# The opening loads of a two-layer encoder kernel: a part of their own behind a barrier, or the head of SyncE's main program

## The reference

```python
def trunk(x, mem, weights):
    for l in range(DEPTH):                                   # 2 layers
        y = parallel_mixer(x, pos, w_in[l], ...)             # windowed attention beside an mLSTM
        x = layer_norm(ALPHA * x + y, ln1_g[l], ln1_b[l])
        y = memory_cross_attention(x, mem, wq_mem[l], wkv_mem[l], wo_mem[l])
        x = layer_norm(ALPHA * x + y, ln2_g[l], ln2_b[l])
        y = grouped_moe(x, router_w, router_bias, w_gate[l], w_up[l], w_down[l])
        x = layer_norm(ALPHA * x + y, ln3_g[l], ln3_b[l])
    return x

def parallel_mixer(x, pos, w_in, ...):
    u = x @ w_in                                             # 1024 -> 2832 columns
    aq, ak, av = u[..., :512], u[..., 512:640], u[..., 640:768]
    ...                                                      # gates: the last 16 columns
```

## Time and profile before

| | |
|---|---|
| executions | 2495.45, 2500.0, 2500.74 us |
| median | 2500.0 us |
| profiled execution | 2492.09 us, of which the span from the first to the last instruction is 2490.4 us |
| PE busy | 2198.6 us (88%) |
| DVE busy | 1317.7 us (53%) |
| ACT busy | 989.8 us (40%) |
| DMA over the span | 386.56 MB, mean 155 GB/s |

### The profile page before, as it was taken

How to read it: one execution, slowest core, us unless ns; L and a number is a source line. 1 busy time by engine, 2 the same in 40 slices (tenths; PEclk the granted TensorE clock), 3 DMA queues, 4 the chain that set the end, 5 groups by cost and what they waited for, 6 DMA issues and landing times.

```text
span 2490.4 us, 35127 instructions
## 1 busy us (share of the span) xinstructions
PE 2198.6 (88%) x13178; PEld 1861.2 (75%) x13178; DVE 1317.7 (53%) x2054; ACT 989.8 (40%) x1642; POOL 199.4 (8%) x241
## 2 busy tenths in 40 slices
PE   5799898998988779999698989899898887999993
PEld 5778875988878757777587887598887875777772
DVE  2476367452153556556767726845215445665567
ACT  2255466223231335455334536622324123554552
POOL 0000011000000222000200000100000022210004
PEclk9899998999998689999899999899999877999997
DMA  3531121122100469999611112023210036999995
GB/s 146 203 106 35 35 85 38 66 102 68 65 29 26 163 239 371 377 382 372 226 60 34 35 35 85 24 80 102 68 51 35 26 132 228 372 378 382 378 369 199
DMA packets 78244, 386.56 MB, mean 155 GB/s; under 512 B 10393, under 2 KB 11433, under 8 KB 43305
## 3 DMA queue, kind: packets, MB, share of 16 engines
q1 hardware_dynamic: 54608, 327.70, 35.1%
q0 software_dynamic: 10448, 31.44, 3.5%
q10 hardware_dynamic: 13064, 25.75, 2.8%
HBM read 338.78 MB, written 46.07 MB: 155 GB/s over the span
## 4 chain that ended last, share of the span: by engine, by line
PE 74%; DVE 14%; ACT 6%; issue 3%; DMA 2%; ACTq 0%; POOL 0%; DVEq 0%; POOLq 0%
PE bank L1923 35%; PE bank L2341 9%; PE bank L2315 8%; PE bank L2305 7%; PE bank L1939 2%; PE bank L2050 2%; PE bank L2221 2%; DVE weight_slots_parts L1292 2%; PE bank L2290 1%; PE bank L2040 1%; ACT weight_slots_parts L855 1%; PE bank L2069 1%; PE bank L2254 1%; ACT x_transposed L995 1%; PE bank L2180 1%
## 5 line engine op out<-in xcount | busy, mean ns | idle before, releaser
L1923 PE MATMUL bank<-weight_slots_parts,x_transposed_parts 128*128 128x256 f32 x2496 | 469.7, 290 | 14.2 <-ACT mixer_region L918 13.9
L1923 PEld LDWEIGHTS bank<-weight_slots_parts,x_transposed_parts 128*128 128x128 f32 x2496 | 401.6, 198 | 15.9 <-ACT mixer_region L918 15.1
L1729 DVE TENSOR_TENSOR weight_slots_parts<-weight_slots,mixer_region_parts 128x2048 fp32r<-128x2048 f32 x140 | 323.7, 2331 | 85.7 <-ACT mixer_region_parts L1129 85.5
L1292 DVE TENSOR_TENSOR weight_slots_parts<-weight_slots,weight_slots_parts 128x2048 fp32r<-128x2048 f32 x58 | 132.9, 2292 | 300.7 <-ACT weight_slots_parts L855 300.2
L1923 PE MATMUL bank<-x_transposed_parts,weight_slots_parts 128*128 128x256 f32 (+1 forms) x1024 | 267.0, 349 | 24.4 <-issue 13.2
L1129 ACT ACTIVATE mixer_region_parts<-weight_slots 128x2048 fp32r<-128x2048 f32 x140 | 261.0, 1909 | 20.5 <-ACT x_transposed L1196 18.2
L2341 PE MATMUL bank<-weight_slots,x_transposed 128*128 128x512 f32 x560 | 246.4, 593 | 0.0
L1923 PEld LDWEIGHTS bank<-x_transposed_parts,weight_slots_parts 128*128 128x128 f32 x1024 | 183.9, 197 | 48.5 <-issue 14.5
L2315 PE MATMUL bank<-mixer_region_parts,x_transposed_parts 128*128 128x256 f32 x1120 | 207.7, 283 | 1.2 <-DVE weight_slots_parts L1729 1.2
L2305 PE MATMUL bank<-mixer_region_parts,x_transposed_parts 128*128 128x512 f32 x560 | 196.0, 422 | 4.2 <-DVE x_transposed_parts L1734 4.2
L2341 PEld LDWEIGHTS bank<-weight_slots,x_transposed 128*128 128x128 f32 x560 | 103.4, 190 | 117.9 <-issue 101.7
(11 more groups left out here) (274 smaller groups left out, 3672.8 us busy)
## 6 DMA issues: line engine op xcount, KB each, us to landing
weight_slots<-in_w_gate SPq DMA_DIRECT2D x70, 1024.0 KB, 7.3
weight_slots<-in_w_up SPq DMA_DIRECT2D x70, 1024.0 KB, 7.0
weight_slots<-in_w_down SPq DMA_DIRECT2D x70, 1024.0 KB, 7.7
weight_slots<-in_w_in SPq DMA_DIRECT2D x20, 1024.0 KB, 5.1
slots_y<-x_transposed ACTq DMA_DIRECT2D x70, 256.0 KB, 7.2
weight_slots<-in_wkv_mem SPq DMA_DIRECT2D x16, 1024.0 KB, 4.9
slots_y<-mixed SPq DMA_DIRECT2D x2, 6912.0 KB, 33.3
weight_slots<-in_w_out SPq DMA_DIRECT2D x8, 1024.0 KB, 4.9
```

Of the source, the lines that this page charges most:

```text
L1292: v.tensor_tensor(half_lo(name), half_raw(name), half_hi(name).bitcast(F32), ALU.subtract).then_inc(w_lo, 1)
L1729: v.tensor_tensor(lo, raw, hi.bitcast(F32), ALU.subtract).then_inc(moe.low_ready, 1)
L1923: ins = pe.matmul(ps, lhs[i](k), rhs[j](k), start=k == 0 and a == 0, stop=k == ks - 1 and a == 2)
```

## The change

The block `start` is gone with its barrier. SP's main program begins with the loads, and POOL's with the memset. The first load is the identity alone, with a semaphore of its own; then chunk 0 of x alone, the kvg weights, chunk 1 of x, q0, q1, chunks 2 and 3, chunks 4 and 5, mk0, the rest of the constants, and the router's two. DVE waits for the rows of ACT's loads only behind the low parts of chunk 0, kvg, chunk 1, q0 and q1. In layer 0 PE takes the steps in another order (`FIRST[0]`): turn 0, turn 1, kvg 0, kvg 1, turn 2, q 0, q 1, turn 3, and from there kvg, q and the turning of the chunk two ahead; in layer 1 the order stays. `tile_plan` walks the same lists. The wait for q0 and the wait for q1 stand each before their own half.

```diff
+FIRST = ([("xn", 0), ("xn", 1), ("kvg", 0), ("kvg", 1), ("xn", 2), ("q", 0), ("q", 1), ("xn", 3)]
+         + [e for c in range(2, NC) for e in ([("kvg", c), ("q", c)] + ([("xn", c + 2)] if c + 2 < NC else []))],
+         [e for c in range(NC + 1) for e in ([("xn", c)] if c < NC else []) + ([("kvg", c - 1), ("q", c - 1)] if c else [])])
...
-        with nc.Block() as start:
-            @start.sync
+        with nc.Block() as block:
+            @block.sync
             def _(sp):
                 now[0] = 0
-                sp.dma_start(cst[:, :], consts[:, 0:C_ALL]).then_inc(consts_loaded, 16)
-                xp_src = x_prompt[0].rearrange("(c p) d -> p c d", p=P)
-                x_src = (xp_src[:, 0:2, :], xp_src[:, 2:4, :], x_sample[0].rearrange("(c p) d -> p c d", p=P))
-                sp.dma_start(x[:, 0:2, :], x_src[0]).then_inc(x_in[0], 16)
+                x_src = x_prompt[0].rearrange("(c p) d -> p c d", p=P)
+                sp.dma_start(cst[:, 0:P], consts[:, 0:P]).then_inc(ident_loaded, 16)
+                sp.dma_start(x[:, 0, :], x_src[:, 0, :]).then_inc(x_in[0], 16)
                 sp.dma_start(kvg_raw, by_k(w_kvg[0])).then_inc(kvg_loaded, 16)
+                sp.dma_start(x[:, 1, :], x_src[:, 1, :]).then_inc(x_in[1], 16)
                 load_half(sp, 0, "q0")
-                sp.dma_start(x[:, 2:4, :], x_src[1]).then_inc(x_in[1], 16)
                 load_half(sp, 0, "q1")
-                sp.dma_start(x[:, 4:6, :], x_src[2]).then_inc(x_in[2], 16)
+                sp.dma_start(x[:, 2:4, :], x_src[:, 2:4, :]).then_inc(x_in[2], 16)
+                sp.dma_start(x[:, 4:6, :], x_sample[0].rearrange("(c p) d -> p c d", p=P)).then_inc(x_in[3], 16)
                 load_half(sp, 0, "mk0")
+                sp.dma_start(cst[:, P:C_ALL], consts[:, P:C_ALL]).then_inc(consts_loaded, 16)
...
-            @start.gpsimd
-            def _(pool):
-                nc.gpsimd.memset(zero_rows, 0.0).then_inc(zeros_made, 1)
-
-        with nc.Block() as block:
-            @block.sync
-            def _(sp):
...
                     if l == 0:
-                        dve.wait_ge(rows_loaded, 4 * 16)
                         for c in range(NC + 2):
...
                             if c == 1:
                                 low_weights("q0")
                                 low_weights("q1")
+                                dve.wait_ge(rows_loaded, 4 * 16)
...
+                    if l == 0:
+                        pe.wait_ge(ident_loaded, 16)
+                    for step_, c in FIRST[l]:
+                        if step_ == "xn":
+                            turn_x(c)
+                        else:
+                            first_products(c, step_)
+                    if l == 0:
+                        pe.wait_ge(consts_loaded, 16)
```

More of the change, by code:

```diff
@@ L187, in keys_of, with tile_plan @@
     return lo, hi - lo + 1, (lo - c + 1) * P
-def tile_plan(used):
+def tile_plan(layer, used):
     place, used, turn = {}, list(used), {}
@@ L199, in tile_plan @@
     every = tuple(range(8))
-    for c in range(NC + 1):
-        if c < NC:
+    for name, c in FIRST[layer]:
+        if name == "xn":
             for h in range(2):
                 add(("xn", c, h), every)
-        if c:
-            add(("kvg", c - 1), every)
-            add(("q", c - 1), every)
+        else:
+            add((name, c), every)
     for k in ("gi", "gf", "gs", "kt0", "kt1"):
@@ L274 @@
 for layer in range(DEPTH):
-    plan, uses = tile_plan(USES_BEFORE_EXPERTS[-1] if layer else [0] * 8)
+    plan, uses = tile_plan(layer, USES_BEFORE_EXPERTS[-1] if layer else [0] * 8)
     TILES.append(plan)
@@ L469, in build_program @@
         gathered = [sem(f"upper_outputs_gathered{c}") for c in range(NC)]
+        ident_loaded = sem("identity_loaded")
         consts_loaded = sem("constants_loaded")
-        x_in = [sem(f"x_loaded{i}") for i in range(3)]
+        x_in = [sem(f"x_loaded{i}") for i in range(4)]
         router_loaded = sem("router_loaded")
@@ L701, in _ @@
             def _(pool):
+                nc.gpsimd.memset(zero_rows, 0.0).then_inc(zeros_made, 1)
                 for l in range(DEPTH):
@@ L876, in _ @@
                         split("mk0")
+                        act.wait_ge(consts_loaded, 16)
                     drain_copy(("gi",), rows[:, 0, 0:512], 512, 8)
@@ L1318, in _ @@
                         low_weights("mk0")
+                        dve.wait_ge(consts_loaded, 16)
                     else:
@@ L1946, in product, with turn_x @@
                         done(ins, key)
[L1949 to L1962, removed]
+                    def turn_x(c):
+                        if l:
+                            pe.wait_ge(x_out, 6 * l - 6 + c + 1)
+                        else:
+                            pe.wait_ge(x_in[min(c, 2 + c // 4)], 16)
+                        for h in range(2):
+                            turn4(("xn", c, h), lambda k: x[:, c, (4 * h + k) * P:(4 * h + k + 1) * P])
@@ L1963, in _, with first_products @@
+                    def first_products(c, part):
+                        tokens_of = by_token(c, lambda k: x_lo[:, c, k, :])
+                        if part == "kvg":
+                            tile_drained(pe, ("xn", c, 0))
+                            tile_drained(pe, ("xn", c, 1))
                             unit_ready("kvg")
-                            key = ("kvg", cc)
+                            key = ("kvg", c)
                             ps = take(key)
                             done(three(ps[:, 0:KVG], tokens_of, (lambda k: kvg_hi[:, k, :], lambda k: kvg_lo[:, k, :])), key)
+                        else:
+                            key = ("q", c)
+                            ps = take(key)
+                            unit_ready("q0")
+                            three(ps[:, 0:HALF_UNIT], tokens_of, columns("q0"))
@@ L1967, in _ @@
                             unit_ready("q1")
-                            key = ("q", cc)
-                            ps = take(key)
-                            three(ps[:, 0:HALF_UNIT], tokens_of, columns("q0"))
                             done(three(ps[:, HALF_UNIT:512], tokens_of, columns("q1")), key)
+                    if l == 0:
[3 more added lines that the diff above has]
+                            turn_x(c)
+                        else:
+                            first_products(c, step_)
```

## The result

The changed kernel took 2476.44 us in the median of four executions (2472.84 to 2480.45), the kernel before 2500.37 (2495.45 to 2502.11): ratio 0.9908, 95% interval 0.9887 to 0.9929. Timed once more later, with other executions of both, it took 2477.99 against 2497.11 us: ratio 0.9928 (0.9912 to 0.9944), or 18 us by the ratio. The two intervals overlap at 0.9912 to 0.9929, 18 to 22 us.

What follows compares the result with a forecast made beforehand. The prediction took waits to bound the first 31.6 us and PE the opening after that. An earlier kvg 0 (17.6 us) and a removed pause (0.6) gave 18.2 us less, taken as 2480 us, range 2471 to 2490.

Steps and rivals of the forecast that it cites:

- What bounded the opening: Start of the kernel: waits bound the first 31.6 us, SP's load issue and barrier, then norm gains; PE bound to 91.0.
- kvg's landing: First kvg weights land at 9.3 us; bounds 7.4 with ACT's loads wholly behind, 9.3 with them wholly ahead.
- The later landings: Opening loads behind kvg, at the latest: chunk 1 at 10.6 us, q0 13.1, q1 15.6, chunks 2 and 3 18.0.
- From the landing to PE: ACT's high part 2.02 us, DVE's low part 2.44, hand-overs about 0.2; kvg 0 begins at 14.0 instead of 31.59.
- The pause before q 0: PE's wait for q1's low part, 37.0 to 37.59 us, goes by the new order of steps: 0.6 us less.
- The slow start of PE: First kvg matmuls at 1.2 GHz: the same 2.5 us charged again; bounds 2.5 us gained or 2.5 lost.
- The sum: Whole opening: 17.6 us from kvg 0's earlier start plus 0.6 from the pause, 18.2 us; bounds 15.7 to 22.6.
- the mark: End of the last q product in layer 0's opening: forecast at about 73 us instead of 91.0.
- The time: Whole kernel: 2480 us, taken from 2473.9 by the profiled execution, 2481.8 by the median and 2478.9 by the average.
- A: Rival at the opening loads: full or competing queues make first units land late, 5 to 13 us gained; chance 0.09.
- B: Rival: something other than SP's opening part holds the engines to 20 us, no change, about 2500 us; chance 0.04.
- C: Rival at the first products: PE stays at 1.2 GHz longer, over 2505 us, 2528 at worst; chance 0.03.

Runs made afterwards that it cites:

- block_kept: The changed kernel's new loads, waits and steps, but with the old opening part and its barrier kept: 2491.82 us, ratio 0.9986 to before.
- router_loads_out: The kernel before, barrier kept, with the router's two loads moved behind the barrier to the head of SP's main program: 2493.5 us, ratio 0.9995.
- rows_waited_first: The changed kernel with DVE's wait for ACT's four row loads back ahead of the first low part: 2487.98 us in one execution.
- rows_late: The changed kernel with ACT's six loads issued behind the high part of q1 instead of first: 2478.75 us, ratio 0.9939 to before.
- old_steps: The changed kernel with PE's steps in layer 0 in the order of before: 2480.08 us, ratio 0.9936 to before.
- block_gone_only: The kernel before with only the opening part and its barrier removed; loads, waits and steps in old order: 2485.29 us, ratio 0.9967.
- both: The changed kernel with kvg first in SP's queue and on ACT and DVE, and ACT's six loads behind q1's high part: 2481.24 us, ratio 0.9928.
- gains_late: The changed kernel with only ACT's two norm-gain loads (512 KB) issued behind the high part of q1: 2484.59 us in one execution.
- fillers: The changed kernel with unread identity transposes on PE while it waits for chunks 0 and 1 and ahead of kvg 0: 2477.7 us, ratio 0.9936.

## Why the prediction was right, and where it was off

- **What bounded the opening**: shown. The barrier was passed when SP had issued its last load (block_kept), and the wait for ACT's rows stood behind it (router_loads_out, rows_waited_first).
- **kvg's landing**: forecast 9.3 us, measured 10.40 (10.45 again). This is the term that was mis-sized. The line for SP's queue alone gave 7.4, rows_late 7.89. ACT's queue was charged 1.9 us from the earlier trace rows and cost 2.5, of which 2.1 came with the four small loads, which I had not priced apart. The upper bound was the right choice, and even that was low. The later landings were further off: chunk 1 at 12.3 (10.6 forecast) and q1 at 17.7 (15.6), so DVE ended the low part of q1 at 22.0 and not 20.0. PE came to q 0 at 24.5, and nothing waited.
- **From the landing to PE**: 4.77 us measured, 4.66 forecast.
- **The pause before q 0** went, as forecast, but not by the new order of steps: old_steps has no pause either. The prediction's step that the 0.6 us are what the new order is worth failed: with the old order q 0 came at 20.96, ahead of the low part of q1, and did not wait, since the wait was split. The forecast had left the split out.
- **The slow start of PE**: 2.5 us was charged again, and 2.9 came (kvg 0 and 1 took 8.73 us; at 0.122 us a matmul they would take 5.9). In the repeat of the same kernel they took 7.62, so the term moves by 1 us between executions.
- **The sum**: 17.6 + 0.6 = 18.2 us forecast, 16.4 + 0.6 = 17.0 at the mark. The mark was forecast at about 73 and came at 74.03 and 72.95.
- **The time**: 2480 forecast, 2476.4 measured, and 2478.0 the second time. The 23.9 us of the first comparison are not a second gain: the later medians of before (2495.78, 2495.74, 2497.11) lie 3 to 5 us under the 2500.4 of the first. That the time landed 2 to 4 us from the forecast is in part the choice of 2480 between sums that gave 2474 and 2482.
- **Rivals**: A (a load held up, 5 to 13 us) did happen in part, 1.1 us of it. B and C did not. In C's worst case the sum is off: 56 us at 0.87 us each cost 49 us and not 46, which is the cost of the 432 matmuls alone; nothing rests on it.

What the parts are worth by the mark: the barrier 11.1 us (block_gone_only), and the new loads, waits and steps a further 5.9 on top of it (7.0 by the second execution), but 2.7 with the barrier still there. Of the 5.9 the moved wait for the rows is about 2, the split wait by the rows 1.2 to 1.5, and the order of steps nothing clear of the scatter; the remainder is the loads' order. It was not split further.

**Why the timed gains don't follow the marks.** In several kernels the timed gain is below the gain at the mark: router_loads_out has 5.7 at the mark and at most 4.7 by its interval, block_gone_only 11.1 and 8 by its ratio. The record has each execution's mean granted clock. Within one kernel, the executions with a lower clock are the slower ones: over the 122 executions of the three later comparisons, each taken against the mean of its own kernel, 0.001 less of clock goes with 1.6 us more (standard error 0.13). router_loads_out had 0.0019 less than before in the mean, block_gone_only 0.0013 less. With this taken off, an estimate, the mean gains are 5.7 and 11.0 us (both with a standard error of 0.9), which are the marks' 5.7 and 11.1; the changed kernel's second comparison gives 16.9. `both` comes to 18.6 of its 22.5, so for it the clock is a part of the answer only. What sets the clock of an execution, no run shows.

## What to carry to other kernels

A barrier behind a block of loads waits for the issuing engine. Here SP's last issue, for 8 KB, took 13 to 19 us in every kernel, and ended some 4 us before that load itself landed (20.4 against 24.1 before, 23.8 against 28.1 after). The barrier made that a wait of all engines: put loads at the head of the main program. I read the long issue as a full queue; no run tests that. Before counting on such a gain, look for the wait behind it: in router_loads_out a wait for rows of no hurry kept two thirds of it. And where several waits share one instruction, split them before reordering the work: by the traces, the one moved line did what a new order of steps had been written for. Last, where a gain is under 1% of the time, compare a mark in the trace, over more than one execution, and look at the granted clock of each execution before explaining a time that doesn't follow.

## What the runs showed of the hardware

**Loads of two queues can land in the order of their issue, but need not.** In the changed kernel: sink rows issued 1.41 landed 7.2, kvg 1.87 and 10.4, norm gains 1.89 and 10.7, chunk 1 of x 2.34 and 12.3, the second gains 2.37 and 13.0. In router_loads_out ACT's gains, issued at 6.57 and 7.10, landed at 17.9 and 21.9, ahead of SP's q1 (3.56 and 22.7) and of chunks 4 and 5 (4.11 and 25.2):

```profile
weight_slots<-in_w_in SPq DMA_DIRECT2D x1, 1024.0 KB, 19.1
...
x<-in_x_sample SPq DMA_DIRECT2D x1, 1024.0 KB, 21.1
...
mixer_norm_gains<-in_mlstm_norm_g ACTq DMA_DIRECT2D x1, 256.0 KB, 14.8
```

Still the 256 KB took 14.8 us, against 5.3 before. The prediction cited the Trainium skill ("DMA: Bandwidth & Descriptors", section "Queues, rings and completion order") on engines that take turns between the queues packet by packet. The overtaking in router_loads_out agrees with turns. The order in the changed kernel does not show them, and no run tells when the one holds and when the other.

**Four loads of 28 KB in ACT's queue held up a load of 1 MB by 2.1 us, two loads of 512 KB in packets of 2 KB by 0.4 us** (gains_late, rows_late).

**PE's granted clock outlasted a pause of 3.3 us and fell from 1.00 to 0.50 some half microsecond after PE had started again** (fillers). A group of transposes can raise the pace as well as matmuls: in `both`, kvg 0 began at full pace behind 3.5 us of them.
